# Returning the last expert's rows by one-hot products, gathering the others' earlier, and a staggered last LayerNorm, in a one-core trunk layer

## The reference, cut to what matters

```
gates = sum(one_hot(eidx, 16) * wts)          # 2 of 16 experts per token
for e in range(16):
    he = silu(xt @ w_gate[e]) * (xt @ w_up[e])
    y = y + gates[:, e:e+1] * (he @ w_down[e])
x = layernorm(alpha * x + y, ln2_g, ln2_b)     # width 1024, all float32
```

## Time and profile before

| | us |
|---|---|
| median of 3 runs (lowest to highest) | 1212.85 (1212.13 to 1215.75) |
| the profiled execution: its time | 1213.8 |
| the profiled execution: its span | 1212.0 |
| PE busy in the span | 1120.5 (92%) |
| DVE busy | 955.2 (79%) |
| ACT busy | 637.9 (53%) |

### The profile page before, as it was taken

How to read it: one execution, slowest core, us unless ns; L and a number is a source line. 1 busy time by engine, 2 the same in 40 slices (tenths; PEclk the granted TensorE clock), 3 DMA queues, 4 the chain that set the end, 5 groups by cost and what they waited for, 6 DMA issues and landing times.

```text
span 1212.0 us, 15132 instructions
## 1 busy us (share of the span) xinstructions
PE 1120.5 (92%) x5829; PEld 873.8 (72%) x5829; DVE 955.2 (79%) x1021; ACT 637.9 (53%) x582; POOL 127.3 (10%) x219
## 2 busy tenths in 40 slices
PE   4999999999999999997799999999999999999960
PEld 4986986987798699985667676767766676776640
DVE  3598898889789885556568888888888888888846
ACT  2432433244243236431267777777777777777730
POOL 3120220220212030000210000000000000000012
PEclk9999999999999999998599999999999999999985
DMA  9663874785486395453399999999999999999924
GB/s 214 204 228 124 278 255 138 245 278 201 152 274 224 124 272 178 139 204 109 108 353 366 377 379 388 374 380 379 380 377 379 382 383 379 380 380 380 384 95 107
DMA packets 171323, 331.85 MB, mean 274 GB/s; under 512 B 8394, under 2 KB 45690, under 8 KB 171232
## 3 DMA queue, kind: packets, MB, share of 16 engines
q1 hardware_dynamic: 150624, 263.95, 62.1%
q0 software_dynamic: 20352, 66.41, 16.6%
q10 hardware_dynamic: 272, 0.47, 0.2%
HBM read 294.88 MB, written 36.63 MB: 274 GB/s over the span
## 4 chain that ended last, share of the span: by engine, by line
PE 78%; DVE 11%; DMA 4%; ACT 3%; issue 2%; POOL 1%; SPq 0%; POOLq 0%; DVEq 0%; ACTq 0%
PE bank L724 74%; PE bank L765 3%; DVE lo L1086 3%; DVE cT L1391 2%; DMA x_in<-in_x_prompt_dram 1%; ACT hi L1081 1%; PE bank L975 1%; DVE st L1535 1%; DMA x_slots<-x,slot 1%; POOL x_slots L682 1%; DMA xg_tok<-x_slots 1%; DMA y_back<-y_slots,slot 1%; ACT hi L1225 1%; DVE o_tok L1497 0%; DVE stats L1489 0%
## 5 line engine op out<-in xcount | busy, mean ns | idle before, releaser
L1690 DVE TENSOR_TENSOR mlo<-mraw,mhi 128x2048 fp32r<-128x2048 f32 x192 | 439.4, 2289 | 78.8 <-ACT mhi L1265 75.5
L1265 ACT ACTIVATE mhi<-mraw 128x2048 fp32r<-128x2048 f32 x192 | 367.4, 1915 | 91.7 <-PE bank L724 85.0
L724 PE MATMUL bank<-mhi,xg_hi 128*96 128x512 f32 x512 | 203.0, 396 | 1.4 <-DVE xg_lo L1695 1.4
L724 PE MATMUL bank<-mhi,xg_lo 128*96 128x512 f32 x512 | 202.7, 396 | 0.0
L724 PE MATMUL bank<-mlo,xg_hi 128*96 128x512 f32 x512 | 201.5, 394 | 0.0
L1081 ACT ACTIVATE hi<-raw 128x2048 fp32r<-128x2048 f32 x47 | 89.9, 1914 | 195.0 <-PE bank L724 167.5
L1086 DVE TENSOR_TENSOR lo<-raw,hi 128x2048 fp32r<-128x2048 f32 x56 | 128.3, 2291 | 78.6 <-ACT hi L1081 43.5
L724 PE MATMUL bank<-xT_hi,hi 128*128 128x336 f32 x512 | 166.0, 324 | 3.1 <-DVE lo L1086 1.7
L724 PE MATMUL bank<-xT_hi,lo 128*128 128x336 f32 x512 | 163.9, 320 | 0.0
L724 PE MATMUL bank<-xT_lo,hi 128*128 128x336 f32 x512 | 163.8, 320 | 0.0
L1391 DVE SCALAR_TENSOR_TENSOR cT<-W,vec,cT 128x336 f32<-128x336 f32 x240 | 118.6, 563 | 0.0
(11 more groups left out here) (253 smaller groups left out, 1496.6 us busy)
## 6 DMA issues: line engine op xcount, KB each, us to landing
mraw<-in_w_gate_dram SPq DMA_DIRECT2D x64, 1024.0 KB, 11.4
mraw<-in_w_up_dram SPq DMA_DIRECT2D x64, 1024.0 KB, 11.3
mraw<-in_w_down_dram SPq DMA_DIRECT2D x64, 1024.0 KB, 12.0
raw<-in_w_in_dram SPq DMA_DIRECT2D x40, 1024.0 KB, 6.7
st<-in_state_ret_dram POOLq DMA_DIRECT2D x32, 512.0 KB, 5.0
out_dram<-st POOLq DMA_DIRECT2D x32, 512.0 KB, 4.5
raw<-in_w_ret_o_dram SPq DMA_DIRECT2D x8, 1024.0 KB, 5.4
x_slots<-zeros POOLq DMA_DIRECT2D x12, 512.0 KB, 4.2
```

Of the source, the lines that this page charges most:

```text
L724: i = pe.matmul(out, a, b, start=s, stop=e)
L1265: act.activation(mhi[:, v % MH, :], mraw[:, v % MR, :], ACT.Copy).then_inc(mhi_ready, 1)
L1690: dve.tensor_tensor(mlo[:, v % MH, :], mraw[:, v % MR, :], mhi[:, v % MH, :].bitcast(f32), ALU.subtract).then_inc(mlo_ready, 1)
```

## The change

It has five parts.

- **The last expert leaves the tables.** `y_slots` is gathered only for experts 0 to 14. DVE splits slots and weights once (`apart`, called in the first expert at `u == 6`): `early_slot` and `early_w` are zero where the token's expert is 15, `last_w` is the weight of expert 15. It makes `picks` anew, a matrix of 112 by 96 per tile that holds `last_w` where a token has that row of expert 15, and `diag`, two diagonal matrices with `early_w` of tile 2. PE transposes `picks` in front of expert 14, ACT copies the result to `back`.
- **The gathers move forward.** POOL issues them once the last weight unit has landed (`mraw_full[MR - 1]`) and, for tiles 1 and 2, once `mlo` of the units whose buffers they overwrite is made.
- **The sum moves in part to PE.** A stage `FIN` with six PSUM banks: for each tile and half, `ident` times `y` (`carried`), for tile 2 also `diag` times the two gathered rows, then `back` times `yo` of expert 15. DVE adds the gathered rows for tiles 0 and 1 only.
- **The last norm is staggered.** Its statistics are read from PSUM, ACT applies scale and shift from PSUM to `y`, DVE multiplies with `ln2_g` a stage later (`gain`). Tile 2 goes out in two halves.
- **`ln2_g` and `ln2_b`** are loaded before the experts.

The diff, cut (`...` marks what is left out):

```diff
-        LAST = Stage(PAIR, expert_groups(0, 1) + expert_groups(1, 0))
+        LAST = Stage(PAIR, ["Pback"] + expert_groups(0, 1) + expert_groups(1, 0))
+        FIN = Stage(LAST, ["Ff00", "Ff01", "Pf10", "Pf11", "Ff20", "Ff21"])
...
 (SP, behind the first eight weight units)
+            sp.dma_start(ln2_bc[:, 0, :], ln2_g.to_broadcast([TT, D])).then_inc(s_ln2, 16)
+            sp.dma_start(ln2_bc[:, 1, :], ln2_b.to_broadcast([TT, D])).then_inc(s_ln2, 16)
...
-            sp.wait_ge(moe_done, 1)
-            sp.dma_start(ln2_bc[:, 0, :], ...)
-            sp.dma_start(ln2_bc[:, 1, :], ...)
...
-                    sp.wait_ge(normed, NT)
+                    for n in range(2):
+                        sp.wait_ge(normed, NT + n)
+                        sp.dma_start(y_prompt[0, a:a + TT, 512 * n:512 * n + 512], y[:, t, 512 * n:512 * n + 512]).then_inc(out_sem, 16)
...
 (POOL)
-                for p in range(2):
-                    stored(LAST, p, 0)
-                    pool.dma_start(y_slots[(NE - 2 + p) * CAP:(NE - 1 + p) * CAP, :], yo[:, p, :]).then_inc(yo_stored, 16)
-                pool.wait_ge(yo_stored, 16 * NE)
+                stored(LAST, 0, 0)
+                pool.dma_start(y_slots[(NE - 2) * CAP:(NE - 1) * CAP, :], yo[:, 0, :]).then_inc(yo_stored, 16)
+                pool.wait_ge(yo_stored, 16 * (NE - 1))
+                pool.wait_ge(early_ready, 1)
+                pool.wait_ge(group_done, LAST.done("xt01"))
+                pool.wait_ge(mraw_full[MR - 1], 12 * NE // MR * 16)
                 for t in range(NT):
+                    if t:
+                        pool.wait_ge(mlo_ready, U_PAIR.idx(15 + t, NE // 2 - 1) + 1 + MLEAD)
                     for k in range(2):
-                        pool.indirect_dma_start(y_back[:, 2 * t + k, :], None, y_slots, ...)
+                        o = y_back12[:, 2 * (t - 1) + k, :] if t else y_back0[:, k, :]
+                        pool.indirect_dma_start(o, None, y_slots[0:(NE - 1) * CAP, :], ...)
...
 (PE)
+                def carried(t):
+                    for n in range(2):
+                        pe.matmul(bank[FIN.bank[f"f{t}{n}"]][0:TT, :], ident[0:TT, 0:TT], y[:, t, 512 * n:512 * n + 512], start=True, stop=False)
...
+                turn(LAST, "back", 0, [(bank[...][0:CAP, t * TT:(t + 1) * TT], picks[:, t, :], TT) for t in range(NT)])
                 expert(LAST, 0, 0, NE // 2 - 1, True)
                 expert(LAST, 1, 0, NE // 2 - 1, False)
+                for t in range(NT):
+                    if t < NT - 1:
+                        pe.wait_ge(summed, t + 1)
+                        carried(t)
+                    else:
+                        pe.wait_ge(diag_ready, 1)
+                        pe.wait_ge(gathered[t], 32)
+                        carried(t)
+                        for n in range(2):
+                            for k in range(2):
+                                pe.matmul(bank[...], diag[:, k, :], y_back12[:, 2 * (t - 1) + k, 512 * n:512 * n + 512], start=False, stop=False)
+                    for n in range(2):
+                        evacuated(LAST, f"d1{n}", 0)
+                        pe.matmul(bank[...], back[:, t * TT:(t + 1) * TT], yo[:, 1, 512 * n:512 * n + 512], start=False, stop=True).then_inc(group_done, 1)
...
 (ACT, per tile)
+                    act.activation(mmv[:, t, 3:4], mmv[:, t, 2:3], ACT.Sqrt).then_inc(rstd_done, 1)
+                    act.wait_ge(shift_ready, t + 1)
+                    for n in range(2):
+                        act.activation(y[:, t, 512 * n:512 * n + 512], b[0:TT, :], ACT.Identity, scale=mmv[:, t, 3:4], bias=mmv[:, t, 1:2]).then_inc(y_scaled, 1)
...
 (DVE)
+                row_stats(0)
+                shift(0)
+                row_stats(1)
+                gain(0)
+                shift(1)
+                row_stats(2)
+                gain(1)
+                shift(2)
+                gain(2)
```

More of the change, by code:

```diff
@@ L1302, in _ @@
                         expert(PAIR, p, it, it, True)
+                b, e = full(LAST, "back")
+                act.activation(back[:, :], b[0:CAP, 0:T], ACT.Copy).then_inc(e, 1)
                 expert(LAST, 0, 0, NE // 2 - 1, True)
                 expert(LAST, 1, 0, NE // 2 - 1, False)
+                for t in range(NT):
+                    act.wait_ge(rv_ready, NORMS + 2 + NT + t)
+                    act.activation(mmv[:, t, 3:4], mmv[:, t, 2:3], ACT.Sqrt).then_inc(rstd_done, 1)
+                    act.wait_ge(shift_ready, t + 1)
+                    for n in range(2):
+                        b = bank[FIN.bank[f"f{t}{n}"]]
+                        act.activation(y[:, t, 512 * n:512 * n + 512], b[0:TT, :], ACT.Identity, scale=mmv[:, t, 3:4], bias=mmv[:, t, 1:2]).then_inc(y_scaled, 1)
             with act.Else():
@@ L1620, in layernorm @@
                 link(i)
-                dve.tensor_tensor(x[:, t, :], x[:, t, :], bc[:, 1, :], ALU.add).then_inc(ready, 1)
+                dve.tensor_tensor(x[:, t, :], x[:, t, :], bc[:, 1, :], ALU.add).then_inc(ready, 2 if ready is normed else 1)
             for n in range(2):
@@ L1700, in hidden, with apart @@
                     dve.tensor_tensor(h_tok[:, 512 * n:512 * n + 512], b[0:CAP, :], sgt[:, :], ALU.mult).then_inc(e, 1)
+                def apart():
+                    for k in range(2):
+                        f = gs[:, 1 + k, :]
+                        link(dve.tensor_tensor(last_w[:, k, :], gt[:, 3 * k + 3, :, NE - 1], gs[:, 3 + 2 * k, :], ALU.mult))
+                        link(dve.scalar_tensor_tensor(early_w[:, k, :], f, float((NE - 1) * CAP), gs[:, 3 + 2 * k, :], ALU.is_lt, ALU.mult))
+                        link(dve.scalar_tensor_tensor(f, f, float((NE - 1) * CAP), f, ALU.is_lt, ALU.mult))
+                    dve.tensor_copy(early_slot[:, :, :], gs[:, 1:3, :]).then_inc(early_ready, 1)
+                    for k in range(2):
+                        i = dve.tensor_scalar(diag[:, k, :], ident[0:TT, 0:TT], early_w[:, k, NT - 1:NT], None, ALU.mult)
+                    i.then_inc(diag_ready, 1)
+                    link(dve.tensor_tensor(last_w[:, 0, :], last_w[:, 0, :], last_w[:, 1, :], ALU.add))
+                    for t in range(NT):
+                        dve.tensor_scalar(picks[:, t, :], row[:, :], rank[:, 1, t:t + 1], last_w[:, 0, t:t + 1], ALU.is_equal, ALU.mult).then_inc(back_ready, 1)
                 def expert(stage, p, it, wit, following):
@@ L1706, in expert @@
                             lo_of(v + u, wit)
+                        if stage is PAIR and it == 0 and p == 0 and u == 6:
+                            apart()
                         if u == 5:
@@ L1736, in _ @@
                 expert(LAST, 1, 0, NE // 2 - 1, False)
[L1737 to L1741 removed]
+                for t in range(NT - 1):
                     dve.wait_ge(gathered[t], 32)
                     for k in range(2):
[L1744 to L1745 removed]
+                        src_ = y_back12[:, 2 * (t - 1) + k, :] if t else y_back0[:, k, :]
+                        i = dve.scalar_tensor_tensor(y[:, t, :], src_, early_w[:, k, t:t + 1], y[:, t, :], ALU.mult, ALU.add)
+                        if k == 0:
+                            link(i)
+                        else:
+                            i.then_inc(summed, 1)
@@ new lines, in _, with row_stats @@
+                dve.wait_ge(s_ln2, 32)
+                def row_stats(t):
+                    for n in range(2):
+                        b, e = full(FIN, f"f{t}{n}")
+                        link(dve.bn_stats(mst[:, t, 6 * n:6 * n + 6], b[0:TT, :]))
+                    link(dve.bn_aggr(mmv[:, t, 0:2], mst[:, t, 0:12]))
+                    link(dve.tensor_scalar(mmv[:, t, 2:3], mmv[:, t, 1:2], EPS, None, ALU.add))
+                    dve.reciprocal(mmv[:, t, 2:3], mmv[:, t, 2:3]).then_inc(rv_ready, 1)
@@ new lines, in shift, with gain @@
+                def shift(t):
+                    dve.wait_ge(rstd_done, NORMS + 1 + NT + t + 1)
+                    dve.scalar_tensor_tensor(mmv[:, t, 1:2], mmv[:, t, 0:1], -1.0, mmv[:, t, 3:4], ALU.mult, ALU.mult).then_inc(shift_ready, 1)
+                def gain(t):
+                    for n in range(2):
+                        c = slice(512 * n, 512 * n + 512)
+                        dve.wait_ge(y_scaled, 2 * t + n + 1)
+                        i = dve.tensor_tensor(y[:, t, c], y[:, t, c], ln2_bc[:, 0, c], ALU.mult)
+                        if t == NT - 1:
+                            link(i)
+                            i = dve.tensor_tensor(y[:, t, c], y[:, t, c], ln2_bc[:, 1, c], ALU.add)
+                        if t == NT - 1 or n:
+                            i.then_inc(normed, 1)
```

57 lines of the change are left out of this document (32 added, 25 removed).

## The result

| | before | after |
|---|---|---|
| median, four runs of each on one chip | 1212.74 (1212.13 to 1215.75) | 1197.31 (1194.21 to 1199.97) |
| ratio, 95% interval | | 0.987 (0.984 to 0.989) |
| profiled execution: time / span | 1213.8 / 1212.0 | 1194.92 / 1193.1 |
| stage | 560.6 | 561.0 |
| tail | 42.25 | 26.55 |

The stage runs from the start of the first product with `xg_lo` to the start of the last expert product; the tail runs from 0.23 behind that start to the end of the span.

The account below looks back on a forecast made before the run. The bound was the 42.3 us tail behind PE's last matmul: gathers, sums, norms, output. PE's end 1185.3 + 11.5 norm and output + 0.5 expert stage = 1197.3 span; + 1.8 - 0.95 = 1198.2 us, range 1194.0 to 1202.5.

Parts of the forecast that it names:

- Gathers shut out by `mlo`: Late in the expert stage: a POOL gather does not get past a running `mlo` and ends 0.8 us after it.
- The fourth gather: Meets the last `mlo`, gets in between DVE's sum instructions at 1167.5, ends at 1168.3; `summed` for tile 1 at 1174.9.
- the lower bound: No exclusion, four sums of 1.3 us from 1166.2: `summed` for tile 1 at 1171.4, PE's end at 1183.6.
- Products: In the tail, 16 float32 products of 512 columns on PE at 0.86 us each, ending at 1185.3.
- Norm of tile 2: Behind PE's end: statistics, shift and gain of tile 2, with `gain(2)` ending at 8.0 us, 1.64 of exclusion included.
- The exclusion by POOL: In the last norm, POOL's addition for tile 1 holds up DVE's `gain(2)` by 1.64 us; bounds 0 and 1.64.
- Output: From DVE's last instruction to the span's end: 3.55 us, against 4.55 before, the last piece being half as large.
- I add nothing: Tile 1's output, started 5.3 us behind PE's end, is through before the last half starts at 8.0: no cost.
- Expert stage: Cost inside the experts, 0.5 us together: 0.3 for DVE's thirteen small instructions, 0.25 for PE's three transposes, the rest 0.
- Sum: Whole kernel: 1185.3 + 11.5 + 0.5 = 1197.3 us span, 14.7 less than 1212.0; time 1198.2.
- No exclusion: Rival: DVE and POOL do not hold each other up; PE ends at 1183.6, tail 9.9, time 1194.8; chance 0.20.
- The clock: Rival: PE's granted clock falls to half as it waits in the tail, 10.4 us more, time 1208.6; chance 0.05.

Follow-up runs that it names:

- e1: Changed kernel with `gain(1)` placed ahead of `row_stats(2)` on DVE; measured 1191.66 us, tail 23.3.
- e2: Changed kernel without POOL's addition of `ln2_b` to tile 1, which SyncE then stores behind `normed`; measured 1195.2 us, tail 23.4.
- e3: Changed kernel with the gathers made to wait for expert 15's last product; measured 1209.98 us, tail 39.5.
- e7: Changed kernel with VectorE's block `apart()` run ahead of the expert loop instead of inside the first expert; measured 1196.93 us, tail 28.3.
- e11: Changed kernel with the last norm not staggered: all statistics, then all shifts, then all gains; measured 1202.57 us, tail 33.9.
- e6: Changed kernel with VectorE also adding tile 2's gathered rows, TensorE's four diagonal products dropped and the norm reordered; measured 1199.2 us, tail 25.9.

## Why the prediction was right, step by step

- **Gathers shut out by `mlo`.** Right, with the very 0.8. The Trainium skill (SBUF — State Buffer, section "Who interferes with whom") has it that an instruction of VectorE with two SBUF inputs shuts out one of GpSimd that reads SBUF, and the trace agrees: held gathers took 1.89 to 2.46 here. Its sentence marked as inferred, on the writing of descriptors, I took to free the gathers, and they were not free. It need not be wrong for that: a gather also reads its row numbers from SBUF, and a plain DMA of POOL went through beside an `mlo` in 0.51.
- **The fourth gather.** This step failed: I had it behind the last `mlo` and between the sums. It started together with that `mlo` and went through, so `summed` for tile 1 came 2.3 behind TensorE's first product (1168.89), not 5.2. This is no luck of one execution. In eleven traces with remainders of full length the gather held by the `mlo` before starts within 0.04 of the last one, since that one starts 1.09 behind its forerunner's end and the gather 0.8 and 0.3 behind it. The forecast's own 1163.9 met an `mlo` of 1163.90 and was read as inside it. The way in that I allowed only between the sums was also too late: the fifth gather, held by the last `mlo`, ended 0.78 behind it although the sum of tile 0 followed at once. TensorE never waited, the lower bound: 13.9 from the first product's start (1166.58) to the last one's end (1180.50), 1.6 less than the 15.6 forecast.
- **Products.** 0.86 each was exact: 16 in 13.76.
- **Norm of tile 2.** 7.64 for 8.0. The exclusion by POOL was predicted at 1.64 and is 1.36, shown by `e1` and `e2`. It holds up VectorE but not the span, which ends with POOL.
- **Output.** The mis-sized term, 5.0 for 3.55, and the wrong path. The 4.55 of the kernel before was taken for output and made shorter with the last piece. But its outputs were through 3.3 behind VectorE's last instruction, and its span, too, ended with POOL's DRAIN. "I add nothing" for tile 1's output was no mistake: in the changed kernel the outputs are through 2.9 behind VectorE. What was missing is POOL's addition for tile 1, which the forecast had end 5.24 behind TensorE: with the 7.45 of its DRAIN before the change and 0.2 to the end that makes 12.9, and 12.6 was measured.
- **Expert stage.** 0.5 forecast, 0.4 found, but not of the parts named. About 0.4 lie in its first 18 us: TensorE was granted 0.51 of its clock in the first 4 us, against 0.61 before. VectorE's block held `h_tok` up by 0.86 and one `mlo` by 0.17 rather than 0.2 to 0.3, while the wait for the second expert's tokens, which I had not treated as a quantity that varies, was 1.5 in the one trace and 0 in the other. This agreement is luck in good part.
- **Sum.** Tail 26.5, within the 24 to 31 set; -1.6, -0.4 and +1.4 make the difference to the forecast's 27.1. Two errors of the forecast, TensorE's wait and the end, nearly cancel; that the time came so near its middle is luck to this extent.
- **Rivals.** "No exclusion" came nearest in its number for TensorE's end, but for another reason; the four gathers of 1.89 to 2.46 speak against its mechanism. The clock did not fall: TensorE had no gap. In `e3`, where it had one of 10.6, it did.

## What to carry to other kernels

A tail behind the last matmul is best attacked by asking what of it does not need the last result: 13 of 15.7 us came from moving six gathers ahead of it. Behind the last tile's chain look for what really ends last: here it was the engine with the longest closing instruction, so its last small addition belongs early (`e1`, 3.2 us) or, which no run here tries, on another engine. When an engine's work is moved forward, check against what it now waits for (here a weight load that had not moved). And with executions 5 us apart, compare stretches of the trace first, then time the winners together.

## What the hardware showed unexpectedly

- POOL's closing DRAIN ends 7.37 us behind the end of its last addition, in thirteen traces out of thirteen, whatever the other engines do. SyncE's ends 2.7 to 3.5 behind the issue of the last output.
- A gather's fate is decided in its first 0.1 us: started within 0.04 us of an `mlo`'s start it takes 0.92, started 0.08 after it 3.04 (`e7`).
- A plain DMA of POOL that starts 0.22 into an `mlo` takes 0.51, as ever.
- The hold works both ways. POOL's addition, begun 0.83 earlier, keeps a 512-column `tensor_tensor` of VectorE at 2.05 instead of 0.69, until 0.55 after POOL's end. Where VectorE's gains lie close together, POOL's addition grows too: 2.65 and 2.71 in `e11`, 2.72 in `e6`, 2.33 to 2.35 elsewhere. A `bn_stats` from PSUM is not held.
- ScalarE's scale and shift from PSUM, 112 by 512, is 0.77 to 0.78 in all six, against 0.59 by the mean for the `yo` copies of 96 by 512.
- TensorE's granted clock stood under full in some executions and not in others at the same place of the same program: 0.91 and 1.00 in the window from 540 to 560, and 1.6 us with it.
